# A decoder step on one core: the output projection cut in two halves, one among attention's steps, the other by thirds of the tokens

## The chip, the cores and the metric

One Trainium2 chip, one of its cores. A core has TensorE (PE, with its weight load PEld), VectorE (DVE), ScalarE (ACT), GpSimd (POOL) and SyncE (SP), which here only issues transfers. The metric is the time of one execution on the device, in microseconds. The inputs are in the chip's memory before it starts, the outputs there when it ends.

## The reference

One layer of a decoder for 1,024 prompt tokens with 16 learned tokens in front, and for 8 sequences that each add one token to 1,024 cached ones. All are computed together as T = 1,048 tokens of D = 2,048 channels, in float32.

```python
def rmsnorm(x, g):
    y = xf * lax.rsqrt(jnp.mean(xf * xf, axis=-1, keepdims=True) + RMS_EPS)
    return y * g
# h = h + W_out [ pool_branch(n) ; attn_branch(n) ],  n = RMSNorm(h), and at the end a final RMSNorm
u, z_pool, q, k, v, z_attn, qi, ki, wi = jnp.split(hn @ w_in, cuts, axis=-1)
# pool branch: (mean of the last 2/4/8/16 of u) - u, per group a linear map, scale, * silu(z_pool)
# attention branch: indexer scores pick 256 keys for each query; softmax over these with a penalty that
# grows with distance; output * silu(z_attn).  8 heads of 128, 2 groups of keys and values
y = rmsnorm(h + jnp.concatenate([pool, attn], -1) @ w_out, final_norm_g)
```

The two halves of the operand of w_out, 1,024 rows each, come from the pool branch (done long before attention) and from attention. The outputs are y, the new keys and values, and the new state of the pool branch.

## The kernel before

The tokens are 9 tiles of 128 (the last has 24: 16 of the prompt, 8 samples). Each engine runs a list of instructions of its own, written by hand; they wait for each other by counting semaphores (`wait_ge`). Nothing is scheduled by a compiler: the order in the text is the order on the engine.

**Split products.** A float32 product is made of three: every weight w is split in whi (by ACT, `split_hi`, L313) and the rest wlo (by DVE, `split_lo`, L323), every operand likewise in hi and lo, and PE adds whi x hi, whi x lo and wlo x hi. A projection goes by blocks of 128 output channels: SP loads a block of weights in two halves of 512 KB (wraw, a ring of 4), `project` (L331) runs its 16 steps of 128 input channels, `step` (L346) its three products for three chunks of tokens (350, 350, 348). That is 144 matmuls a block, gathered in three PSUM banks; ACT copies them to stage (`evacuate`, L486) and stores them in memory.

**Stages in order of time.** Input norm and the turning of x into ahi and alo, with two chunks of projection block 0 among the tiles by the table `EARLY` (L362); the indexer's queries, the indexer with main blocks among its heads; the main blocks, beside which DVE picks the top 256 keys; keys and values turned; prompt attention; attention of the 8 samples over cached pages; output projection; last norm. The part of PE's time up to 1270 us is, apart from the start, not touched.

**Prompt attention.** 18 units (`AUNITS`: tiles 8 to 0, key groups 0 and 1) of 4 heads, so 72 heads k. For head k PE computes the scores (`scores`, L1647 and L1666: three products per chunk, up to 1,040 keys), DVE adds bias and mask and finds the maximum (L1335) into a buffer prob (NPROB = 3 of them), ACT takes the exponential (L996), DVE or ACT divides. LAG = 7 heads later come its turned blocks: PE transposes 4 heads x 128 keys (L1700), ACT copies them to pts (L984), PE weighs the values with them (`weighted`, L1670, L1680, two PE passes a block) into out_bank(v), one of two banks, and DVE multiplies the unit's sum by the gate (`gate`, L1311). `back_blocks` (L514) says which blocks fall to which head. Keys and values are copied from PSUM into one tile each, kvtok (L1296), by ACT and DVE in turn.

**Output projection.** SP loads the operand's 16 rows of blocks back from memory (mix_scratch) into orow; ACT (`operand_hi`, L1006, L1009) and DVE (`operand_lo`, L1360, L1362) split them into oparts, 4 among the samples' steps, 12 after. Then 16 blocks: 144 matmuls, ACT's evacuation (L496, L498), PE's turning of the block before (`turn_h`, L1778: 8 transposes L1789 and 1 L1794), DVE's addition of x (`add_residual`, L1392), ACT's squares (L1043), and the store of h in memory (h_scratch). After the last block: DVE's roots, a reload of h, nine multiplications by root and weight (L1476) and the stores (L1099).

**Pages.** The samples' cached pages are loaded by SP (even halves) and POOL (odd halves) by `load_keys` and `load_values` (L466, L472); keys go to PSUM and are turned (L1729), scored (L1740), then softmax (exponential L1027), the turning of it (L1746) and the weighing of values (L1769).

## Time and profile before

| | |
|---|---|
| Median of three runs | 1995.37 us (1994.33, 1995.37, 1997.87) |
| Profiled execution | 1997.71 us |
| Its span, first to last instruction | 1996.0 us |
| Mean granted TensorE clock | 0.979 |
| Busy: PE, DVE, ACT, POOL | 94%, 47%, 29%, 11% |
| Moved by DMA over the whole span | 198.96 MB, 100 GB/s |

The profiled execution is one of its own. "Busy" is the time in which at least one instruction is under way on an engine; matmuls are pipelined, so that a PE which is always busy may still issue at less than its pace. The pace is read from the starts of instructions in a row. A row of the timeline groups equal instructions that follow each other; the time in square brackets is the idle time ahead of it and the instruction that ended it.

### The profile page before, as it was taken

What the parts mean: (1) busy time and instruction counts of PE and PEld (TensorE: products, weight loads), DVE (VectorE), ACT (ScalarE), POOL (GpSimd) and SP (SyncE); (2) the same over time, 40 slices, a digit from 0 to 9 for tenths busy, and PEclk for the clock granted to TensorE, in tenths of its full rate; (3) what the DMA queues carried; (4) which work ended last, traced back from release to release, by engine and by line L of the source; (5) the groups of instructions that cost most, each with busy time, mean ns of one, the idle gap of its engine ahead of it and who ended that gap; (6) DMA issues with size and microseconds to landing.
All of it is one profiled execution on the core that took longest, in us unless ns stands there. A gap on an engine that the chain in (4) does not pass through costs nothing.

```text
span 1996.0 us, 28168 instructions
## 1 busy us (share of the span) xinstructions
PE 1874.3 (94%) x11014; PEld 1702.9 (85%) x11014; DVE 941.1 (47%) x1549; ACT 582.6 (29%) x1094; POOL 221.6 (11%) x227
## 2 busy tenths in 40 slices
PE   5999989998999999999999999899988999999993
PEld 4899977867999999999999999666554699999993
DVE  7401038874666565556565656654542211111115
ACT  6211136751111221111111111466653312222221
POOL 5200000004000000314151610110012000000000
PEclk9999989999999999999999999999999999999996
DMA  6232133213222221323232322423348323333338
GB/s 214 57 90 75 53 85 84 67 35 96 83 75 66 64 74 55 122 76 116 82 112 85 112 85 86 128 73 92 93 139 267 107 66 86 85 85 87 94 95 341
DMA packets 245917, 198.96 MB, mean 100 GB/s; under 512 B 25332, under 2 KB 228028, under 8 KB 243507
## 3 DMA queue, kind: packets, MB, share of 16 engines
q1 hardware_dynamic: 214541, 134.51, 23.9%
q10 hardware_dynamic: 25990, 49.64, 6.7%
q0 software_dynamic: 5312, 13.83, 2.2%
q8 instruction: 45, 0.74, 0.2%
q14 instruction: 29, 0.24, 0.0%
HBM read 146.94 MB, written 51.46 MB: 99 GB/s over the span
## 4 chain that ended last, share of the span: by engine, by line
PE 83%; DVE 6%; ACT 4%; issue 2%; DMA 2%; SPq 1%; POOL 0%; DVEq 0%; ACTq 0%; POOLq 0%
PE ps L354 68%; PE ps L1680 3%; PE ps L1666 2%; PE ps L1549 2%; DVE score L1196 2%; PE ps L1740 2%; PE ps L1769 2%; ACT pts L984 1%; PE ps L1700 1%; PE ps L1620 1%; DVE fh L1476 1%; DVE alo L1121 1%; PE ps L1729 1%; ACT wraw L852 1%; PE ps L1789 1%
## 5 line engine op out<-in xcount | busy, mean ns | idle before, releaser
L328 DVE TENSOR_TENSOR wlo<-wraw,whi 128x1024 fp32r<-128x1024 f32 (+1 forms) x122 | 160.5, 1317 | 745.2 <-ACT whi L320 744.9
L354 PE MATMUL ps<-ahi,whi 128*128 128x350 f32 (+3 forms) x2160 | 474.2, 326 | 5.3 <-DVE wlo L328 3.0
L354 PE MATMUL ps<-alo,whi 128*128 128x350 f32 (+3 forms) x2160 | 471.4, 324 | 0.0
L354 PE MATMUL ps<-ahi,wlo 128*128 128x350 f32 (+3 forms) x2160 | 470.3, 323 | 0.0
L354 PEld LDWEIGHTS ps<-ahi,whi 128*128 128x128 f32 (+1 forms) x2160 | 367.3, 189 | 9.4 <-ACT stage L498 3.0
L354 PEld LDWEIGHTS ps<-alo,whi 128*128 128x128 f32 (+1 forms) x2160 | 368.5, 189 | 0.5
L354 PEld LDWEIGHTS ps<-ahi,wlo 128*128 128x128 f32 (+1 forms) x2160 | 367.7, 189 | 0.6
L354 PE MATMUL ps<-oparts,whi 128*128 128x350 f32 (+1 forms) x1536 | 290.5, 324 | 0.0
L320 ACT ACTIVATE whi<-wraw 128x1024 fp32r<-128x1024 f32 (+1 forms) x122 | 128.5, 1055 | 476.3 <-PE ps L354 379.4
L354 PEld LDWEIGHTS ps<-oparts,whi 128*128 128x128 f32 x1536 | 252.5, 189 | 1.1 <-DVE oparts L1362 0.2
L496 ACT ACTIVATE stage<-ps 128x700 f32<-128x700 f32 (+1 forms) x61 | 46.1, 756 | 611.9 <-PE ps L354 611.9
L1224 DVE MATCH_REPLACE8 score<-m,score 128x640 f32<-128x640 f32 (+6 forms) x224 | 204.3, 924 | 0.0
L1214 DVE MAX8 m<-score 128x8 f32<-128x640 f32 (+6 forms) x224 | 191.8, 927 | 16.1 <-POOL score L1838 15.8
L354 PE MATMUL ps<-oparts,wlo 128*128 128x350 f32 (+1 forms) x768 | 165.3, 323 | 0.0
L354 PEld LDWEIGHTS ps<-oparts,wlo 128*128 128x128 f32 x768 | 130.7, 189 | 0.0
L1680 PE MATMUL ps<-pts,kvtok 128*128 128x512 f32 (+1 forms) x180 | 85.9, 559 | 15.2 <-ACT pts L984 14.9
L1335 DVE CUSTOM_DVE_ANT_0 prob<-score,ps 16x1040 f32<-16x1040 f32 (+6 forms) x56 | 52.4, 935 | 71.3 <-PE ps L1666 71.1
L1549 PE MATMUL ps<-khi,qst 128*128 128x512 f32 (+3 forms) x208 | 62.7, 368 | 16.6 <-ACT wraw L852 10.8
L1196 DVE SCALAR_TENSOR_TENSOR score<-wraw,wsc,score 128x384 f32<-128x384 f32 (+6 forms) x56 | 56.0, 999 | 13.8 <-ACT wraw L852 9.7
L436 POOL DMA_DIRECT2D iload<-cache_idx_k x32 | 17.4, 546 | 403.0 <-issue 402.5
L1549 PEld LDWEIGHTS ps<-khi,qst 128*128 128x128 f32 (+1 forms) x208 | 31.8, 169 | 34.8 <-ACT wraw L852 14.3
L1196 DVE SCALAR_TENSOR_TENSOR score<-relub,wsc,score 128x384 f32<-128x384 f32 (+6 forms) x56 | 56.0, 999 | 10.6 <-ACT relub L852 5.8
(186 smaller groups left out, 1628.1 us busy)
## 6 DMA issues: line engine op xcount, KB each, us to landing
wraw<-w_in SPq DMA_DIRECT2D x88, 512.0 KB, 3.8
proj_scratch<-stage ACTq DMA_DIRECT2D x44, 524.0 KB, 2.7
wraw<-w_out SPq DMA_DIRECT2D x32, 512.0 KB, 6.1
orow<-mix_scratch SPq DMA_DIRECT2D x16, 524.0 KB, 5.8
xt<-x_prompt SPq DMA_DIRECT2D x7, 1024.0 KB, 4.9
xblk<-x_prompt SPq DMA_DIRECT2D x16, 448.0 KB
h_scratch<-hblk ACTq DMA_DIRECT2D x14, 512.0 KB
fh<-h_scratch SPq DMA_DIRECT2D x8, 896.0 KB, 11.2
```

Source lines behind the costliest of these rows:

```text
L320: nc.scalar.activation(whi[:, s, :, 0:width], wraw[:, 2 * p + s, :, 0:width], ACT.Copy).then_inc(S["w_hi"], 1)
L328: nc.vector.tensor_tensor(wlo[:, s, :, 0:width], wraw[:, 2 * p + s, :, 0:width], whi[:, s, :, 0:width].bitcast(F32), ALU.subtract).then_in ...
L354: last = nc.tensor.matmul(ps[0:width, 3 * pair(n) + c, 0:tn], w[:, s, k, 0:width], m[:, a, t0:t0 + tn], start=(a == 0 and w is whi and m i ...
L496: nc.scalar.activation(stage[0:width, p, 0:700].rearrange("p (c t) -> p c t", c=2), ps[0:width, b:b + 2, 0:350], f, scale=scale)
L1196: nc.vector.scalar_tensor_tensor(out=out, in0=relu_of(u)[0:rows, 0:keys_of(i)], scalar=wsc[0:rows, i, 8 * h + k:8 * h + k + 1], in1=out, o ...
L1214: x = nc.vector.max(m8[0:r, m, :], score_of(t)[0:r, :])
L1224: x = nc.vector.match_replace(score_of(t)[0:r, :], m8[0:r, m, :], score_of(t)[0:r, :], NEG_TAKEN)
L1335: nc.vector.tensor_tensor_reduce(x, dist_of(i)[0:n, :], psf[0:n, o:o + w], 1.0, NEG_TAKEN, ALU.add, ALU.max, peak).then_inc(S["abias"], 1)
L1549: last = nc.tensor.matmul(psf[0:rows, o + c:o + c + cw], qst[:, n % 2, k, 0:rows], m[:, c:c + cw], start=m is khi, stop=m is klo)
L1666: last = nc.tensor.matmul(psf[0:n, o + c:o + c + cw], q[:, qbuf(u), 4 * g + r, 0:n], m[:, g, c:c + cw], start=m is akh and q is qh, stop=q ...
L1680: nc.tensor.matmul(ps[:, out_bank(v), 0:4 * n], kvtok[0:kn, j, 256 + 128 * g:256 + 128 * g + 128], pts[0:kn, t % 2, 0:4 * n], start=j == 0 ...
L1740: nc.tensor.matmul(psf[0:64, c:c + w], q, skt[:, (m - 1) % 2, c:c + w], start=m == 1, stop=m == NSAMP * KVH)
```

## The change

**Start.** `EARLY` now puts two of three chunks of projection blocks 0 and 1 among tiles 3 to 9, and their third chunks behind the last tile. DVE and ACT split block 1 at tiles 4 and 5; block 0 has its split weights in buffers of its own (khi0, klo0).

```diff
-        EARLY = {3: (0, 0, 6), 4: (0, 6, 11), 5: (0, 11, 16), 6: (1, 0, 6), 7: (1, 6, 11), 8: (1, 11, 16)}
+        EARLY = {3: [(0, 0, 0, 6)],
+                 4: [(0, 0, 6, 11)],
+                 5: [(0, 0, 11, 16), (1, 0, 0, 8)],
...
+                 9: [(1, 1, 11, 16)]}
```

**First half of the output projection.** The rows of the pool branch (opart, 8 steps of 128) times w_out are cut in 384 fills: 16 blocks n x 3 chunks c (384, 384, 280 tokens) x 8 steps k, each three matmuls. 216 stand among the steps of prompt attention from head 8 on, 96 among the samples' steps, 72 behind them beside the split of the late operands. Eight fills make a part; all parts gather in PSUM bank 3, and each is copied by ACT into stage, a block's third part followed by the split of the weights after next and the store in part_scratch. One order for all engines is written by new functions:

```python
        AUNITS = [(i, g) for i in ATILES for g in range(KVH)]
        NHEAD = 4 * len(AUNITS)
        LAG = 6
...
        FILLS = [("fill", n, c, k) for n in range(NOUT) for c in range(len(OUT_CHUNKS)) for k in range(HALF)]
        IN_PROMPT, IN_SAMPLES = 216, 96
        def prompt_order():

            fills = FILLS[:IN_PROMPT]
            first = 8
            cost = [0 if k < first else 350 + (keys_of(AUNITS[k // 4][0]) if k < NHEAD else 100) for k in range(LAST_K)]
            order, waiting, done, t = [], None, 0, 0
            for k in range(LAST_K):
                order.append(("score", k))
                if waiting:
                    order.append(waiting)
                    waiting = None
                if k < HALF:
                    order.append(("operand", k))
                until = len(fills) * sum(cost[:k + 1]) // sum(cost)
                blocks = back_blocks(k)
                here, share = fills[done:until], max(1, len(blocks))
                done = until
                for x in range(share):
                    if x < len(blocks):
                        order.append(("turn", *blocks[x], t))
                    if x == 0:
                        order.append(("soft", k))
                    order += here[x * len(here) // share:(x + 1) * len(here) // share]
                    if x < len(blocks):
                        if waiting:
                            order.append(waiting)
                        waiting = ("weigh", *blocks[x], t)
                        t += 1
            assert not waiting
            return order
...
        def sample_order():

            fills = FILLS[IN_PROMPT:IN_PROMPT + IN_SAMPLES]
            order, done = [], 0
            for count, what in ([(3, ("keys", m)) for m in range(NSAMP * KVH + 1)] + [(17, ("probs", 0)), (4, ("copied", 0))]
                                + [(3, ("values", b)) for b in range(NSAMP)]):
                order += fills[done:done + count] + [what]
                done += count
            return order + fills[done:]

        def last_order():

            fills = FILLS[IN_PROMPT + IN_SAMPLES:]
            order = []
            for k in range(HALF):
                order += [("operand", k)] + fills[k * len(fills) // HALF:(k + 1) * len(fills) // HALF]
            return order
...
        def fill_act(act, n, c, k):

            if k < HALF - 1:
                return
            t0, tn = OUT_CHUNKS[c]
            act.wait_ge(S["o_mm"], 3 * n + c + 1)
            if c == 0 and n < 2:
                act.wait_ge(S["op_lo"], HALF)
            if c == 0 and n >= 2:
                act.wait_ge(S[f"stored{n % 2}"], 16 * (stored_blocks(n % 2) + n // 2))
            nc.scalar.activation(stage[:, n % 2, t0:t0 + tn], ps[:, 3, 0:tn], ACT.Copy).then_inc(S["o_kept"], 1)
            if c == len(OUT_CHUNKS) - 1:
                if n + 2 < NOUT:
                    out_hi(act, n + 2)
                else:
                    late_hi(act, n + 2 - NOUT)
                act.wait_ge(S["o_kept"], 3 * n + 3)
                act.dma_start(part_d[128 * n:128 * n + 128, :], stage[:, n % 2, :]).then_inc(S[f"stored{n % 2}"], 16)
...
        def fill_pe(pe, n, c, k):

            t0, tn = OUT_CHUNKS[c]
            if c == 0 and k == 0:
                pe.wait_ge(S["ow_lo"], n + 1)
            if n == 0 and c == 0:
                pe.wait_ge(S["op_lo"], k + 1)
                pe.wait_ge(S["abias"], 8)
            elif k == 0:
                pe.wait_ge(S["o_kept"], 3 * n + c)
            for w, x in ((whi, 0), (whi, 1), (wlo, 0)):
                last = nc.tensor.matmul(ps[:, 3, 0:tn], w[:, n % 2, k, :], opart[:, k, x, t0:t0 + tn],
                                        start=k == 0 and w is whi and x == 0, stop=k == HALF - 1 and w is wlo)
            if k == HALF - 1:
                last.then_inc(S["o_mm"], 1)
```

In attention the scores of even heads lie in banks 0 and 1 and those of odd heads in banks 4 and 5 (`score_bank`; only tile 8's 1,040 keys reach 16 columns into bank 2 or 3), the out bank is one (bank 2), the turned blocks use banks 6 and 7, prob has two buffers (NPROB = 2), the lag is 6. Blocks fall to three of a unit's four heads, and `gate(v)` stands in head 4 v + 10.

```diff
-                if j == 0 and v > 1:
-                    pe.wait_ge(S["gated"], v - 1)
+                if j == 0 and v:
+                    pe.wait_ge(S["gated"], v)
...
-                nc.tensor.matmul(ps[:, out_bank(v), 0:4 * n], kvtok[0:kn, j, 256 + 128 * g:256 + 128 * g + 128],
+                nc.tensor.matmul(ps[:, 2, 0:4 * n], vtok[0:kn, j, 128 * g:128 * g + 128],
```

The operand's eight rows are loaded and split in heads 0 to 7. Turned keys and values are copied by two instructions a tile, and the first two weight halves are split before the first head. Cached pages have whole tiles for themselves: the even samples come by SP, the odd by POOL, keys 0 and 1 early, the other keys and the values once all of attention's weighings are done.

The rows below are PE's order in prompt attention. Before, with kvtok for keys and values, pts the turned blocks and akh, qh the split keys and queries (L1700 turns, L1680 weighs, L1666 scores):

```order
3003 L1680 MATMUL ps<-pts,kvtok 128x512 [waits gated,pt_copied]
3004 L1700 MATMUL ps<-cst,prob 128x128 [waits pt_copied]
3005 L1700 MATMUL ps<-cst,prob 128x128 x3
3006 L1700 MATMUL ps<-cst,prob 128x128 [waits pt_copied]
3007 L1700 MATMUL ps<-cst,prob 128x128 x3
3008 L1680 MATMUL ps<-pts,kvtok 128x512 [waits pt_copied]
3009 L1666 MATMUL ps<-akh,qh 128x512 [waits abias]
```

PE in the same stage after the change (L1896 turns, L1910 weighs, L1882 scores, L695 is a fill; o_kept counts the parts that ACT has copied out of bank 3):

```order
2909 L1896 MATMUL ps<-cst,prob 128x128 [waits pt_copied]
2910 L1896 MATMUL ps<-cst,prob 128x128 x3
2911 L695 MATMUL ps<-opart,whi 128x384 x2
2912 L695 MATMUL ps<-opart,wlo 128x384
2913 L695 MATMUL ps<-opart,whi 128x384 x2
2914 L695 MATMUL ps<-opart,wlo 128x384
2915 L695 MATMUL ps<-opart,whi 128x384 [waits o_kept]
2916 L695 MATMUL ps<-opart,whi 128x384
2917 L695 MATMUL ps<-opart,wlo 128x384
2918 L1910 MATMUL ps<-pts,vtok 128x512 [waits gated,pt_copied]
2919 L1882 MATMUL ps<-akh,qh 128x512 [waits abias]
```

Between the transposes and the weighing stand fills now; the third of them is the first of a new part and waits for the copy of the part that ended one row before.

DVE at the first heads of attention, before (L1296 copies turned keys and values, L1335 is bias and maximum, prob its result):

```order
307 L1296 COPY kvtok<-ps 128x512 [waits kv_turned] x4
308 L1335 ISA prob,ast<-score,ps 16x1040 [waits aqk,dist_masked]
309 L1335 ISA ast 16x1
310 L1338 TENSOR_SCALAR ast<-ast 16x1 [waits abias]
311 L1335 ISA prob,ast<-score,ps 16x1040 [waits aqk]
312 L1335 ISA ast 16x1
```

and after (L631 is the weights' lower half, L1524 the operand's, L1570 bias and maximum):

```order
315 L1516 COPY vtok<-ps 128x256
316 L631 TENSOR_TENSOR wlo<-wraw,whi 128x1024 [waits ow_hi] x2
317 L1524 TENSOR_TENSOR opart<-stage,opart 128x1048 [waits op_hi,dist_masked]
318 L1570 ISA prob,ast<-score,ps 16x1040 [waits aqk]
319 L1570 ISA ast 16x1
320 L1573 TENSOR_SCALAR ast<-ast 16x1 [waits abias]
321 L1524 TENSOR_TENSOR opart<-stage,opart 128x1048 [waits op_hi]
322 L1570 ISA prob,ast<-score,ps 16x1040 [waits aqk]
```

One operand split stands ahead of each of the first heads' maxima.

**Second half.** The rows of attention (oattn) times w_out go by 48 parts: for each third of the tokens (384, 384, 280) all 16 blocks, 24 matmuls each, with the weights of a half block loaded again for each third (ring of 4). The stores and reloads of h are gone: DVE adds the first half's part (`join`), PE turns three transposes, DVE adds the result to x, which is already in fh; squares, roots, scaling and stores of a third run in the next third, those of the last behind the end.

```python
        def late_weights(q, j):

            if j < 2:
                q.wait_ge(S["ow_lo"], NOUT - 1 + j)
            elif j < 4:
                q.wait_ge(S["sv_used"], 3)
            else:
                q.wait_ge(S["lw_lo"], j - 3)
            n = j % NOUT
            q.dma_start(wraw[:, j % 4, :, :],
                        w_out[0, POOLW:D, 128 * n:128 * n + 128].rearrange("(k p) n -> p k n", p=128)
                        ).then_inc(S[f"w_in{j % 4}"], 16)
...
            for j in range(PARTS):
                c, n = divmod(j, NOUT)
                join(j)
                if j + 2 < PARTS:
                    late_lo(dve, j + 2)
                if j:
                    add_residual(j - 1)
                if c and n == 4:
                    moments(c - 1)
                if c and 5 <= n <= 7:
                    finish(3 * (c - 1) + n - 5)
            add_residual(PARTS - 1)
            moments(2)
            for i in tiles_of(2):
                finish(i)

...
            for j in range(PARTS):
                t0, tn = OUT_CHUNKS[j // NOUT]
                pe.wait_ge(S["lw_lo"], j + 1)
                if j >= 3:
                    pe.wait_ge(S["l_kept"], j - 2)
                for k in range(HALF):
                    if j == 0:
                        pe.wait_ge(S["oa_lo"], k + 1)
                    for w, x in ((whi, 0), (whi, 1), (wlo, 0)):
                        last = nc.tensor.matmul(ps[:, j % 3, 0:tn], w[:, j % 2, k, :], oattn[:, k, x, t0:t0 + tn],
                                                start=k == 0 and w is whi and x == 0, stop=k == HALF - 1 and w is wlo)
                    if k == 3 and j:
                        turn_h(j - 1)
                last.then_inc(S["l_mm"], 1)
            turn_h(PARTS - 1)
```

The end of PE's list before (L354 are the projection's matmuls, L1789 and L1794 turn the block before, stage holds what was evacuated):

```order
3799 L354 MATMUL ps<-oparts,wlo 128x348
3800 L1792 REGISTER_ALU
3801 L1794 MATMUL ps<-cst,stage 24x128 [waits h_part]
3802 L1805 REGISTER_ALU
3803 L1805 COMPARE_AND_BRANCH
3804 L1789 MATMUL ps<-cst,stage 128x128 [waits h_added,evac]
3805 L1789 MATMUL ps<-cst,stage 128x128 x7
3806 L1794 MATMUL ps<-cst,stage 24x128 [waits h_part]
```

and a part near the end after (L2024 the matmuls of a part, L2012 the transposes of the part before; lw_lo counts split weights, l_kept joined parts):

```order
5148 L2024 MATMUL ps<-oattn,whi 128x280 [waits l_kept,lw_lo]
5149 L2024 MATMUL ps<-oattn,whi 128x280
5150 L2024 MATMUL ps<-oattn,wlo 128x280
5151 L2024 MATMUL ps<-oattn,whi 128x280 x2
5152 L2024 MATMUL ps<-oattn,wlo 128x280
5153 L2024 MATMUL ps<-oattn,whi 128x280 x2
5154 L2024 MATMUL ps<-oattn,wlo 128x280
5155 L2024 MATMUL ps<-oattn,whi 128x280 x2
5156 L2024 MATMUL ps<-oattn,wlo 128x280
5157 L2012 MATMUL ps<-cst,stage 128x128 [waits h_added,l_kept]
5158 L2012 MATMUL ps<-cst,stage 128x128
5159 L2012 MATMUL ps<-cst,stage 24x128
5160 L2024 MATMUL ps<-oattn,whi 128x280 x2
```

A part waits only for its split weights and for the join of three parts before.

## Rows read from the trace of the kernel before

**Rows 1.** The page: span, and busy time of each engine.
```profile
span 1996.0 us, 28168 instructions
...
PE 1874.3 (94%) x11014; PEld 1702.9 (85%) x11014; DVE 941.1 (47%) x1549; ACT 582.6 (29%) x1094; POOL 221.6 (11%) x227
```
**Rows 2.** Windows: stretch, us, PE, PEld, DVE, ACT, POOL busy, clock, DMA, GB/s.
```profile
1282.90:1301.60 18.70, 16.50 (x99) 8.49 (x97) 16.77 (x40) 14.24 (x24) 6.11 (x12) 0.99 0.66 204
1301.60:1481.70 180.10, 165.09 (x801) 109.03 (x800) 99.05 (x329) 121.28 (x255) 7.26 (x13) 1.00 0.31 86
1481.70:1575.30 93.60, 86.82 (x392) 40.05 (x392) 12.06 (x12) 26.06 (x30) 20.34 (x38) 0.95 0.58 184
1575.30:1960.50 385.20, 385.20 (x2439) 383.60 (x2439) 73.65 (x103) 97.67 (x324) 0.00 (x0) 1.00 0.35 104
1960.50:1996.10 35.60, 1.48 (x10) 0.95 (x9) 23.99 (x27) 7.95 (x40) 0.00 (x0) 0.57 0.85 341
```
**Rows 3.** The chain that ended last: start, us, 72 matmuls of half a block.
```profile
1611.15 11.57 PE ps L354 x72
```
**Rows 4.** Timeline of PE, input stage: start, us, instruction, [idle before <-releaser].
```profile
43.84 1.76 PE L1492 MATMUL ps<-cst,xt 128*128 128x128 f32 x12 [0.35 <-DVE alo L1121]
...
49.36 1.76 PE L1492 MATMUL ps<-cst,xt 128*128 128x128 f32 x12 [0.36 <-DVE alo L1121]
```
**Rows 5.** Timeline of DVE: the first head's maximum, and an operand split.
```profile
1282.86 1.22 DVE L1335 CUSTOM_DVE_ANT_0 prob<-score,ps 16x1040 f32<-16x1040 f32 x1 [3.77 <-PE ps L1666]
...
1526.88 1.25 DVE L1362 TENSOR_TENSOR oparts<-orow,oparts 128x1048 fp32r<-128x1048 f32 x1 [4.64 <-ACT oparts L1009]
```
**Rows 6.** Attention: timelines of PE, ACT and DVE, then PE's grouped rows.
```profile
1323.07 0.57 PE L1666 MATMUL ps<-akh,ql 128*128 128x512 f32 x2
1323.48 1.02 PE L1680 MATMUL ps<-pts,kvtok 128*128 128x512 f32 x2
1324.33 1.04 PE L1700 MATMUL ps<-cst,prob 128*128 128x128 f32 x8
1325.62 1.12 PE L1680 MATMUL ps<-pts,kvtok 128*128 128x512 f32 x2 [0.25 <-ACT pts L984]
...
1322.74 1.15 ACT L1004 ACTIVATE prob<-prob,ast 128x1024 f32<-128x1024 f32 x1
1324.97 1.08 ACT L984 ACTIVATE pts<-ps 128x512 f32<-128x512 f32 x2 [1.08 <-PE ps L1700]
...
1323.67 1.09 DVE L1335 CUSTOM_DVE_ANT_0 prob<-score,ps 128x896 f32<-128x896 f32 x1 [2.49 <-PE ps L1666]
1325.07 0.75 DVE L1309 TENSOR_SCALAR prob<-prob,ast 128x1024 f32<-128x1024 f32 x1
...
L1680 PE MATMUL ps<-pts,kvtok 128*128 128x512 f32 x144 | 78.7, 628 | 13.2 <-ACT pts L984 13.2
L1700 PE MATMUL ps<-cst,prob 128*128 128x128 f32 x288 | 40.1, 273 | 0.0
L1666 PE MATMUL ps<-akh,qh 128*128 128x512 f32 x44 | 25.9, 610 | 0.0
```
**Rows 7.** Timeline of ACT at two places, then PE's waits in the samples' stage.
```profile
1534.25 1.24 ACT L1027 ACTIVATE sprob<-sprob,sst,cst 64x1025 f32<-64x1025 f32 x1 [5.42 <-DVE sst L1371]
1581.17 1.08 ACT L1009 ACTIVATE oparts<-orow 128x1048 fp32r<-128x1048 f32 x1 [1.85 <-DMA orow<-mix_scratch]
...
PE ps L1746 <- DVE sprob L1376: 5.1, 1, 5.1
```
**Rows 8.** Timelines of ACT and DVE in the tail.
```profile
1961.18 0.46 ACT L498 ACTIVATE stage<-ps 128x348 f32<-128x348 f32 x1
...
1970.09 20.44 DVE L1476 SCALAR_TENSOR_TENSOR fh<-fh,fst,fg 128x2048 f32<-128x2048 f32 x9
```
**Rows 9.** DMA queues, 1575 to 1961 us: packets, MB, share of 16 engines.
```profile
q1 hardware_dynamic: 50017, 32.72, 28.8%
```

1123 lines of the change are left out of this document (592 added, 531 removed).

## Prediction

> **What bounds the kernel now.** I read the busy times of the page first: PE is busy for 1874.3 of 1996.0 us, DVE and ACT for 47% and 29% [rows 1]. The change touches what comes after 1282.9 us and the input stage, so I cut the span there by stages [rows 2]. The output projection (1575.3 to 1960.5) has PE busy in all of its 385.2 us, and the tail behind it only for 1.48 of 35.6 us: there is nothing to win in the first but by moving its matmuls under the idle time of other stages, and much in the second. Prompt attention (1301.6 to 1481.7) shows PE at 165.1 of 180.1 us, but a busy PE there is not a full one. The timeline [rows 6] gives true pitches from start to start: four score matmuls (512 and 384 columns twice) begin 0.41 us apart for 896 columns, 0.457 ns a column, so 0.234 us for 512, 0.175 for 384, 0.128 for 280; a weighing (two records of 512) takes 0.85, a transpose record 0.109. By the counts of the grouped rows, 72 weighings are 61, 288 transposes 31, the scores of 512, 384, 256 and 128 columns 31 + 8.4 + 5.6 + 2.8, the small ones of the last tiles 7: 147 us of work in 180, so 33 us are lost. Where: after its last transpose PE waits for ACT's copy (the weighing at 1325.62 comes 0.42 us later than 1324.33 + 8 x 0.109) and restarts slowly. The samples' stage summed likewise has 76 us of work in 93.6, 18 lost, 5.1 of them the wait for the softmax [rows 7]. In the output projection 72 matmuls take 11.57 us [rows 3], or 0.161 each, which is its full pitch. Durations are from the profiled execution, 1997.71 us; the median of the runs is 2.3 lower, and the sum is made against 1997.71.
>
> **The change, part by part.** The count of matmul columns in the output projection does not change: 16 blocks x 16 steps x 3 products x 1048 columns in both, 0.478 us for a step's three products over 350 or so columns, and the three new chunks (0.525 + 0.525 + 0.385) average the same. What changes is what else PE does meanwhile.
>
> (a) *Start.* Before, PE idles between input tiles: two starts of a tile's transposes are 5.5 us apart [rows 4], with 1.76 of transposes and some 2.6 of block 0 in it, so about 1.1 is free in each. The new table puts two thirds of block 1 there (32 steps, 32 x 3 x 0.16 = 15.4 us), more than is free in six tiles (7 us); what doesn't fit lengthens the stage, and the rest comes off behind it. DVE's block 1 split moves too. I take -3, between -5 and +1.
>
> (b) *Keys, values and the first eight heads.* Each turned tile is copied by two instructions instead of one, and four weight splits stand between them and the first head: +2. Then each of the first eight heads gets one operand half-split: 1.08 us on ACT and 1.25 us on DVE [rows 5, 7]. DVE is busy for 16.77 of 18.70 us in this stretch [rows 2], and so it sets the pace: the DVE part stands on the path, 8 x 1.25 = 10, less 1 that fits in its idle time: +9. Together +11; the bounds are +6 (the rest of DVE's idle time and the longer lead of scores take half) and +15 (ACT too, at 14.24, becomes late).
>
> (c) *Rest of attention.* 216 of the 384 fills stand between the turns and the weighings. A fill lasts 0.5 us and the wait it covers 0.42, so the 33 us lost go: -33. In return all fills accumulate in one PSUM bank, so the first fill of each part waits until ACT has copied the part before. There are 27 such places here; in 16 a fill stands right behind a fill, as in the second order excerpt (the wait for o_kept). The copy takes 0.46 us [rows 8], the last matmul's drain and PE's restart about 0.3 more, so 0.7 with ACT free. But ACT is busy for 121.3 of 180.1 us [rows 2], in pieces of 1.15 (exponential) and 1.08 (copy of turned blocks) [rows 6], and each copy has its fixed place in ACT's order: 67% of about 1.1 in front, plus what stands before it in the order. I take 1.7 each, 27 us, and 2 for the 11 separated ones: +29. With one output bank in place of two, the first weighing of a unit also waits for DVE's gating of the unit before, placed in the same head: 17 times about 0.5, as DVE is at 55% here: +8. Sum +4. If ACT is always ahead, it is 16 x 0.7 + 2 x 0 and a hidden gate, -33 + 13 = -20; if each wait takes a whole piece of ACT's work more (2.8), +20.
>
> The order excerpt shows the wait and [rows 2] an ACT that is busy for 67%. The Trainium skill, Perfetto Trace Analysis, section Matmuls, speaks against this change: independent groups of matmuls should rotate through different PSUM banks, so that the evacuation of one overlaps the matmuls of the next, and here the parts share one. By that rule alone the price is one copy and its restart a part, which is rival A's value; no row of before shows either.
>
> (d) *Samples.* 96 fills go among 76 us of work: the 18 lost go, and 12 part ends cost 0.7 each, ACT being nearly idle (26.06 of 93.6 us [rows 2]): +8. One of them stands behind ACT's exponential of the softmax, which waits for DVE: +3. The changed page loads and the start cost +3. Sum -4, between -12 and +6.
>
> (e) *The last nine parts.* 72 fills now stand with eight late operands. 8 boundaries in a row: 8 x 0.7 = 6. The first operand can only be split after the last value matmul, the gated output's way through memory being as long as now (orow lands, ACT waits 1.85, [rows 7]): 7.3 us against 3.8 us of fills that do not wait on ACT, so +4. Sum +10, between +6 and +16.
>
> (f) *The second half by thirds.* 48 parts of 24 matmuls and three transposes, 199 us of PE work in all. The third excerpt shows the only waits: the split weights and the joined part. Per part (4.5 us) ACT has 1.05 and DVE 1.3 of splitting, 0.5 of join and 0.4 of residual; with two or three finishing multiplications of 2.27 (20.44 / 9, [rows 8]) in a third DVE can be late. The queue must bring 25 MB of weights (each half block of 512 KB three times), 8.6 MB of parts and 8.6 MB of x, and beside them 5.7 MB of finished rows go out, less some 2 MB loaded ahead: 46 MB in 199 us, 231 GB/s. The row of the stage now: q1 moves 32.72 MB with 28.8% of 386 us [rows 9], that is 294 GB/s while it moves. It should do, but x's 3.1 MB burst per third stands in front of weights in the same queue (10.6 us against a ring of four parts, 17 us). I take +6, from 0 to +25.
>
> (g) *Tail.* Now 35.6 us, 20.44 of it nine scalings in a row, behind a reload of h [rows 2, 8]. After, three scalings stand there and no reload: -6 x 2.27 = -13.6, and 1.5 for the reload's share: -15, between -12 and -18.
>
> Sum: -3 + 11 + 4 - 4 + 10 + 6 - 15 = **+9**: 2006.7 for a profiled run, 2004 for the median.
>
> **Rivals.** *A, the waits stay small and it is faster.* If PE's deep queue of other work keeps ACT ahead, part ends cost 0.7 and gates nothing: (c) is -20 and (d) -8, and (b) half hidden at +9: -3 + 9 - 20 - 8 + 8 + 4 - 14 = -24, and 7 for late parts, so -17: 1981 profiled, 1978 for the median. For it: PE has 3.4 fills or 1.6 us more in each of 64 heads, so that ACT, with 27 copies and 9 blocks' splits added (121 + 12 + 10 us of some 255), falls from 67% to 56%. Against it: an in-order ACT queue in which the copy stands behind pieces that themselves wait for PE. *B, transfers bound the thirds and it is slower.* If weights arrive at less than 231 GB/s, PE waits for splits in every part; at 200 GB/s 46 MB take 230 us: +31 instead of +6, and so 2029. Against it: 294 GB/s in the row. It decides from 231 GB/s down. *C, DVE rather than PE bounds attention*, as in the first eight heads: DVE's work in the rest is 99 of 180 us [rows 2], plus 14 splits of 1.23 and nothing else, so it does not bind. *D, it does nothing*: the gains and the stalls of (c) cancel with (b) and (g) to under 4 us, as when a part end in attention costs 1.3 us and not 1.7 (16 x 0.4 = 6 us less).
>
> **How the numbers follow.** Forecast (slower by 4 to 20 us, centre 2004) 0.39; A 0.38; B 0.11; D 0.12; C is inside the forecast's bounds. A measurement of this kernel can tell about 0.2%, 4 us, from no change: slower 0.50 (forecast and B), same 0.12 (D), faster 0.38 (A). The range takes in A with 10 us more (d and e at their lower bounds) and so begins at 1968, and B with a queue at 203 GB/s (+28), 2026; outside lie less than 0.1 on either side. The likeliest case by itself spans 1999 to 2016.
>
> **What would show it.** In the trace after: (b) DVE's reductions of the first eight heads 3.4 us apart, not 2.3; (c) PE's first fill of a part idle for ACT's copy, 25 to 30 us in total over attention, and weighings idle for DVE's gate under 10; if the first is under 12, A is right. (e) a gap of 4 us at the first matmul of the second half's operand. (f) PE waiting for wlo, with transfers in flight, only at the starts of thirds; if in each part, B. (g) about 20 us from PE's last matmul to the end. My forecast is wrong if attention's stretch with its fills (147 + 103 us of work) lasts under 260 us, or if the thirds last over 215.

## The result, and the profile after

The changed kernel takes 2032.76 us, the median of four runs (2029.88 to 2034.64), against 1996.62 us for the kernel before in the same comparison: a ratio of 1.0167, with a 95% interval of 1.0149 to 1.0186. It is slower by 36 us. The sign of the forecast was right, but "slower" had been given a chance of 0.50 only. Its size (+9 us on the profiled run, 2004 us) was not right, and the time lies outside the range of 1968 to 2026.

The page of the changed kernel, its span and busy times, which answer to [rows 1]:

```profile
span 2032.9 us, 27737 instructions
...
PE 1887.0 (93%) x11014; PEld 1711.4 (84%) x11014; DVE 1003.9 (49%) x1641; ACT 595.2 (29%) x885; POOL 220.6 (11%) x227
```

The windows of its stages (us, PE, PEld, DVE, ACT, POOL busy, granted clock, DMA share, GB/s) answer to [rows 2]:

```profile
1282.20:1326.30 44.10, 29.48 (x133) 19.43 (x131) 25.01 (x47) 23.22 (x38) 0.00 (x0) 0.69 0.46 146
1326.30:1618.50 292.20, 266.53 (x1426) 213.40 (x1426) 108.72 (x338) 141.00 (x284) 7.32 (x14) 0.99 0.28 80
1618.50:1756.60 138.10, 130.79 (x663) 81.69 (x663) 9.89 (x15) 28.71 (x39) 27.19 (x51) 1.00 0.43 135
1756.60:1800.50 43.90, 36.55 (x217) 34.23 (x218) 12.63 (x13) 13.38 (x18) 0.00 (x0) 1.00 0.58 184
1800.50:2017.60 217.10, 204.32 (x1298) 200.51 (x1296) 119.70 (x175) 67.85 (x69) 0.00 (x0) 0.98 0.73 222
2017.60:2032.90 15.30, 0.03 (x1) 0.00 (x0) 8.65 (x12) 2.37 (x7) 0.00 (x0) 0.64 0.41 150
```

The windows start at the same landmarks as those of before: the first maximum of head 0, the maximum of head 9, the first matmul of the samples' bias, the end of the samples' values, the last fill, PE's last transposes. To compare, the fills in a stretch are taken off at 0.478 us each (there are 4, 218, 90.3 and 71.7 of them in the first four), and the second half is held against what is left of the old projection, 385.2 - 384 x 0.478 = 201.6 us.

| stretch | before | after less fills | difference | forecast |
|---|---|---|---|---|
| to the first turned key | 1270.0 | 1267.9 | -2.1 | (a) -3 |
| to head 0's maximum | 12.9 | 14.3 | +1.4 | (b) +2 |
| heads 0 to 8 | 18.7 | 42.2 | +23.5 | (b) +9 |
| rest of attention | 180.1 | 188.0 | +7.9 | (c) +4 |
| samples | 93.6 | 94.9 | +1.3 | (d) -4 |
| last nine parts | 0 | 9.6 | +9.6 | (e) +10 |
| second half | 201.6 | 217.1 | +15.5 | (f) +6 |
| tail | 35.5 | 15.3 | -20.2 | (g) -15 |
| sum | | | +36.9 | +9 |

The largest row is the first heads (the stretch of 18.7 us in [rows 2] holds nine heads, 0 to 8; the prediction counted eight). From one maximum to the next, heads 0 to 7 took 14.0 us before and 28.0 after, and the step from head 7 to head 8 took 1.8 and 11.4. The chain of work that ended last passes through them as follows (start, us, what):

```profile
1282.36 3.37 DMA stage<-mix_scratch
1285.75 1.09 ACT opart L1193
1286.86 1.25 DVE opart L1524
1288.11 1.14 DVE prob L1570
...
1292.88 1.17 ACT prob L1230
1294.05 0.97 ACT opart L1193
1295.04 1.25 DVE opart L1524
1296.29 1.14 DVE prob L1570
```

It is not DVE's 1.25 us alone that lies on the path, as the prediction had it, but a loop over both engines: DVE's maximum waits in DVE's order for the operand's low half, that for ACT's high half, and that in ACT's order for a normalisation, which waits for DVE. From 1285.75 to head 6's maximum the chain holds five of DVE's subtractions (6.1 us) and three of ACT's copies (3.0 us). Then, from head 7 to head 8, DVE stands for 9.9 us with nothing to do, and PE's clock has fallen. In windows of 5 us of the same kernel (columns as above; the figure third from the end is the granted clock, 0.50 being the lower of its two levels, 1.2 GHz):

```profile
1285.00:1290.00 5.00, 2.50 (x15) 0.89 (x14) 4.17 (x9) 3.84 (x5) 0.00 (x0) 1.00 0.56 157
...
1300.00:1305.00 5.00, 1.00 (x8) 0.92 (x8) 2.77 (x6) 3.48 (x6) 0.00 (x0) 0.50 0.31 107
1305.00:1310.00 5.00, 4.24 (x17) 2.61 (x18) 3.97 (x7) 1.19 (x2) 0.00 (x0) 0.50 0.17 41
1310.00:1315.00 5.00, 3.98 (x21) 3.49 (x20) 1.45 (x4) 2.62 (x6) 0.00 (x0) 0.50 1.09 337
1315.00:1320.00 5.00, 5.00 (x19) 3.89 (x19) 0.00 (x0) 1.58 (x4) 0.00 (x0) 0.50 0.75 263
1320.00:1325.00 5.00, 5.00 (x20) 4.64 (x20) 2.19 (x5) 1.45 (x3) 0.00 (x0) 0.50 0.02 5
```

The kernel before is at 1.00 in all of these windows. In windows of 1 us the fall lies near 1298.4 us, and the clock is back at 1.00 near 1325.7, after 27 us. PE had been busy for a little under half of the 13 us before the fall, and had stood for 3.2 us just ahead of it:

```profile
1297.49 0.65 PE L1882 MATMUL ps<-akh,qh 128*16 128x512 f32 x3 [3.20 <-DVE ast L1570]
...
1297.00:1298.00 1.00, 0.51 (x3) 0.23 (x4) 0.93 (x5) 1.00 (x3) 0.00 (x0) 1.00 0.66 163
1298.00:1299.00 1.00, 1.00 (x7) 0.38 (x6) 1.00 (x2) 1.00 (x2) 0.00 (x0) 0.69 0.90 356
```

The same scores of head 8 in the two kernels, before (L1666) and after (L1882):

```profile
1314.55 0.62 PE L1666 MATMUL ps<-akl,qh 128*128 128x512 f32 x2
1315.01 0.62 PE L1666 MATMUL ps<-akh,ql 128*128 128x512 f32 x2
...
1315.12 1.05 PE L1882 MATMUL ps<-akl,qh 128*128 128x512 f32 x2
1315.97 1.05 PE L1882 MATMUL ps<-akh,ql 128*128 128x512 f32 x2
```

Two matmuls of 512 columns take 0.46 us before and 0.85 after.

Part ends. The timelines of PE and ACT where a part ends with ACT occupied, and where ACT is free:

```profile
1412.22 0.33 PE L695 MATMUL ps<-opart,wlo 128*128 128x384 f32 x1
1412.56 1.03 ACT L1222 ACTIVATE prob<-prob,ast 128x896 f32<-128x896 f32 x1
1413.59 0.48 ACT L659 ACTIVATE stage<-ps 128x384 f32<-128x384 f32 x1
1414.12 0.53 PE L695 MATMUL ps<-opart,whi 128*128 128x280 f32 x2 [1.57 <-ACT stage L659]
...
1796.38 0.34 PE L695 MATMUL ps<-opart,wlo 128*128 128x384 f32 x1
1796.75 0.49 ACT L659 ACTIVATE stage<-ps 128x384 f32<-128x384 f32 x1 [3.60 <-PE ps L695]
1797.30 0.53 PE L695 MATMUL ps<-opart,whi 128*128 128x280 f32 x2 [0.58 <-ACT stage L659]
```

The next fill starts 1.90 us after the last one in the first case and 0.92 in the second, where 0.175 would do: 1.7 and 0.75 us lost. Those are the two values of the prediction (1.7 and 0.7). The mean lies between them: at the 16 places in this stretch where a fill follows a fill across a part end, measured like this, 20.1 us are lost, 1.3 each. The rule that the prediction named (the Trainium skill, Perfetto Trace Analysis, section Matmuls: independent groups should rotate through PSUM banks, so that a copy overlaps the next group's matmuls) agrees with the trace: 0.75 us is lost at a part end even where ACT is free. ACT's own work comes on top of it. PE's waits in the rest of attention, then in the last nine parts (us in total, times, longest):

```profile
PE ps L695 <- ACT stage L659: 22.4, 20, 2.2
PE ps L1910 <- DVE osb L1548: 2.6, 3, 1.3
...
PE ps L695 <- ACT stage L659: 7.4, 8, 3.3
```

(The restart after a wait is not in the idle time.) The single output bank costs 2.6 us, not 8: fills stand in front of that wait too. In the last nine parts one wait of 3.3 us is the late operand's.

Thirds. Parts begin every 4.53 us in the whole second third and every 3.42 us in the last, the pitch of their matmuls. The first third has three parts of 8.73, 11.16 and 7.37 us. What stands there, timelines of PE, DVE and ACT:

```profile
1818.67 0.55 PE L2012 MATMUL ps<-cst,stage 128*128 128x128 f32 x3 [2.45 <-DVE stage L1633]
...
1817.52 0.56 DVE L1645 TENSOR_TENSOR fh<-ps,fh 128x384 f32<-128x384 f32 x1 [5.50 <-DMA fh<-x_prompt]
...
1820.32 1.06 ACT L641 ACTIVATE whi<-wraw 128x1024 fp32r<-128x1024 f32 x1 [9.56 <-DMA wraw<-w_out]
```

x is late for DVE, and the weights behind x for ACT. PE waits only twice for split weights (7.8 us in total), both times in the first third.

### The profile page after: what moved, and what is told of

Its sections match the earlier page's. It is cut to its first block, busy times and chain, and to the rows that moved or that the text cites. A ratio compares the mean times of both kernels' runs of the same rounds, so it can differ in the third digit from the quotient of the medians.

```text
span 2032.9 us, 27737 instructions
## 1 busy us (share of the span) xinstructions
PE 1887.0 (93%) x11014; PEld 1711.4 (84%) x11014; DVE 1003.9 (49%) x1641; ACT 595.2 (29%) x885; POOL 220.6 (11%) x227
## 4 chain that ended last, share of the span: by engine, by line
PE 81%; DVE 6%; ACT 4%; DMA 4%; issue 3%; SPq 2%; POOL 0%; DVEq 0%; ACTq 0%; POOLq 0%
PE ps L350 49%; PE ps L695 9%; PE ps L2024 7%; PE ps L1910 3%; PE ps L1882 3%; PE ps L1770 2%; PE ps L1896 2%; PE ps L1953 1%; DVE score L1415 1%; PE ps L1979 1%; PE ps L1841 1%; ACT stage L659 1%; DMA wraw<-w_out 1%; PE ps L1942 1%; ACT wraw L1063 1%
## 5 line engine op out<-in xcount | busy, mean ns | idle before, releaser
L350 PE MATMUL ps<-ahi,whi 128*128 128x350 f32 (+1 forms) x2112 | 463.8, 326 | 5.1 <-DVE wlo L328 2.7
L350 PE MATMUL ps<-alo,whi 128*128 128x350 f32 (+1 forms) x2112 | 461.5, 324 | 0.0
L350 PE MATMUL ps<-ahi,wlo 128*128 128x350 f32 (+1 forms) x2112 | 460.2, 324 | 0.0
L350 PEld LDWEIGHTS ps<-ahi,whi 128*128 128x128 f32 x2112 | 361.3, 190 | 8.6 <-ACT stage L507 3.0
L350 PEld LDWEIGHTS ps<-alo,whi 128*128 128x128 f32 x2112 | 362.3, 190 | 0.0
L350 PEld LDWEIGHTS ps<-ahi,wlo 128*128 128x128 f32 x2112 | 361.8, 190 | 0.0
L328 DVE TENSOR_TENSOR wlo<-wraw,whi 128x1024 fp32r<-128x1024 f32 x88 | 119.4, 1358 | 448.8 <-ACT whi L319 448.6
L695 PE MATMUL ps<-opart,whi 128*128 128x384 f32 (+1 forms) x768 | 205.0, 352 | 36.1 <-ACT stage L659 36.1
L319 ACT ACTIVATE whi<-wraw 128x1024 fp32r<-128x1024 f32 x88 | 93.3, 1061 | 379.1 <-PE ps L350 358.2
L1433 DVE MAX8 m<-score 128x8 f32<-128x640 f32 (+6 forms) x224 | 191.8, 926 | 16.1 <-POOL score L2058 15.8
L2024 PE MATMUL ps<-oattn,whi 128*128 128x384 f32 (+1 forms) x768 | 187.1, 330 | 7.8 <-DVE wlo L646 7.8
L695 PEld LDWEIGHTS ps<-opart,whi 128*128 128x128 f32 x768 | 128.3, 191 | 56.9 <-ACT stage L659 34.8
L2024 PEld LDWEIGHTS ps<-oattn,whi 128*128 128x128 f32 x768 | 132.5, 190 | 8.7 <-DVE wlo L646 8.5
L1570 DVE CUSTOM_DVE_ANT_0 prob<-score,ps 16x1040 f32<-16x1040 f32 (+6 forms) x56 | 52.3, 934 | 152.5 <-PE ps L1896 92.2
L695 PE MATMUL ps<-opart,wlo 128*128 128x384 f32 (+1 forms) x384 | 124.8, 325 | 0.0
L2024 PE MATMUL ps<-oattn,wlo 128*128 128x384 f32 (+1 forms) x384 | 124.2, 323 | 0.0
L641 ACT ACTIVATE whi<-wraw 128x1024 fp32r<-128x1024 f32 x48 | 50.9, 1061 | 144.1 <-PE ps L2024 119.6
L1910 PE MATMUL ps<-pts,vtok 128*128 128x512 f32 (+1 forms) x180 | 83.1, 545 | 6.6 <-DVE osb L1548 2.6
L631 DVE TENSOR_TENSOR wlo<-wraw,whi 128x1024 fp32r<-128x1024 f32 x16 | 19.5, 1224 | 136.7 <-ACT whi L626 136.7
```

Source lines behind the costliest of these rows:

```text
L319: nc.scalar.activation(hi[:, s, :, 0:width], wraw[:, 2 * p + s, :, 0:width], ACT.Copy).then_inc(S["w_hi"], 1)
L328: nc.vector.tensor_tensor(lo[:, s, :, 0:width], wraw[:, 2 * p + s, :, 0:width], hi[:, s, :, 0:width].bitcast(F32), ALU.subtract).then_inc( ...
L350: last = nc.tensor.matmul(ps[0:width, 3 * pair(n) + c, 0:tn], w[:, s, k, 0:width], m[:, a, t0:t0 + tn], start=(a == 0 and w is hi and m is ...
L641: nc.scalar.activation(whi[:, j % 2, :, :], wraw[:, j % 4, :, :], ACT.Copy).then_inc(S["lw_hi"], 1)
L695: last = nc.tensor.matmul(ps[:, 3, 0:tn], w[:, n % 2, k, :], opart[:, k, x, t0:t0 + tn], start=k == 0 and w is whi and x == 0, stop=k == H ...
L1433: x = nc.vector.max(m8[0:r, m, :], score_of(t)[0:r, :])
```

## The experiments

Seventeen kernels ran beside the kernel before. Times below are medians of four runs; a comparison was made against the kernel before on the same chip, whose median is given with it. That median lies between 1996.6 and 2003.3 us from one comparison to the next. A difference between two changed kernels that were compared apart is therefore good to some 5 us, and small ones are given by their ratios as well (0.001 is 2 us).

### Part ends pulled apart

```diff
-            return order
+            return separated(order)
...
+                if item[0] == "fill":
+                    held.append(item)
+                else:
+                    out.append(item)
+                    since += cost.get(item[0], 0)
+                while held and (held[0][3] or since >= GAP):
+                    out.append(held.pop(0))
+                    since = 0.0
```

(`held[0][3]` is the fill's k, 0 at the start of a part; GAP is 0.8 us; `cost` is 1.0 for scores, 0.85 for a weighing, 0.44 for a turn, 2.0 for page keys and values.)

> The changed kernel with its part ends pulled apart: the first fill of a part is held back until at least 0.8 us of other PE work (scores, turns, weighings, page keys, values) has been issued behind the last fill of the part before; the later fills move with it. Nothing else is changed. Theory (one PSUM bank: PE stands at each part end for ACT's copy and what ACT has queued before it): the stalls between two fills, 37 us in attention and 11 in the samples' stage in the trace of the changed kernel, fall to under half, and the time by 15 to 28 us, to about 2010. Rival (ACT's queue is the limit, so that the wait reappears at the next instruction): under 5 us gained.

2018.47 us, before 1997.61, ratio 1.0097 (1.0075 to 1.0119): 14.3 us less than the changed kernel, just under the expected range. Of this 9.8 us lie between heads 8 and 71. PE's waits for ACT's copy in attention fell from 22.4 us to

```profile
PE ps L712 <- ACT stage L676: 8.8, 14, 1.3
PE ps L1927 <- DVE osb L1565: 7.4, 6, 2.6
```

and some of it came back as the wait for the gate in the second row. The single bank is a cost of the order, more than of the bank.

### The operand's low half on POOL

```diff
-                nc.vector.tensor_tensor(opart[:, k, 1, :], orow1[:, k % 2, :], opart[:, k, 0, :].bitcast(F32),
+                nc.gpsimd.tensor_tensor(opart[:, k, 1, :], orow1[:, k % 2, :], opart[:, k, 0, :].bitcast(F32),
```

> The changed kernel with the eight subtractions that make the low half of the pool operand moved from DVE to POOL, which is idle there. Theory (the 1.25 us on DVE are on the path of the first heads): the step from head to head in heads 0 to 7 falls from 4.0 to about 2.8 us, 8 to 10 us gained there, minus what POOL's slower subtraction holds back (the reload of the next operand row waits for it). Rival (ACT's high halves and the loads set that pace, DVE only waits): under 3 us.

2028.72 us, before 1997.61, ratio 1.0150 (1.0128 to 1.0172), 4 us less, within the two intervals, and far under the 8 to 10 expected. Heads 0 to 7 took 25.9 us and not 28.0, and the step to head 8 stayed at 11.4. The chain shows another loop in the old one's place:

```profile
1286.07 2.44 POOL opart L2099
...
1288.53 3.53 DMA stage<-mix_scratch
...
1292.08 1.08 ACT opart L1193
...
1293.23 2.41 POOL opart L2099
```

The operand's rows pass through two buffers. A new row is loaded only when the subtraction from its buffer is done, and POOL takes 2.4 us for it where DVE took 1.25. The round of subtraction, load and ACT's copy takes 7.2 us for two rows. Up to head 6 this kernel was 6.7 us ahead, then head 7 came 10.5 us behind head 6 and not 5.9: its scores stand in PE's order behind a weighing that waits for ACT's copy of a turned block, and this copy stands in ACT's order behind the operand's, which waits for its row. So this run does not tell DVE's share: it exchanged one loop for another.

### Two buffers in the kernel before

```diff
-NPROB = 3
+NPROB = 2
...
-        LAG = 7
+        LAG = 6
...
-            return [(v, j) for j in quarter(AUNITS[v][0], r)]
+            if v >= len(AUNITS) or r == 3:
+                return []
+            i = AUNITS[v][0]
+            return [(v, j) for j in range(r * (i + 1) // 3, (r + 1) * (i + 1) // 3)]
```

> The kernel before with two prob buffers instead of three, a lag of 6 heads instead of 7, and a unit's turned blocks in three heads instead of four, as the change has it; no fills, no operand work. Theory (head 4u must wait until the unit two before is wholly turned, which ends only in that head): 8 us lost from head 7 to head 8, and some 0.5 to 1.5 us at each of 15 later units: 1996 + 8 + 15 = about 2019, 2010 to 2030. Rival (the two buffers cost nothing by themselves, only beside fills): within 4 us of before.

2011.58 us, before 1997.61, ratio 1.0075 (1.0047 to 1.0103): 14 us slower, inside the expected range. Maximum of head 0 to that of head 8 went from 15.8 to 22.3 us, from there to head 71 from 175.3 to 183.8. DVE's waits in attention show what the buffer does; the first row, for PE's turns, is not there at all in the kernel before:

```profile
DVE prob L1338 <- PE ps L1703: 69.9, 16, 7.9
DVE prob L1338 <- PE ps L1669: 23.4, 19, 3.2
```

Sixteen times DVE cannot begin a unit until PE has turned the unit two before. The edit holds three things, the buffers, the lag and the order of the turns, and they were not run apart. In heads 0 to 8 there is a fourth: after a wait of 1.8 us the clock was at 0.50 here too, from 1295 to 1298 us. The prediction gave NPROB and LAG no term.

### No fills among attention and samples

```diff
-        IN_PROMPT, IN_SAMPLES = 216, 96
+        IN_PROMPT, IN_SAMPLES = 0, 0
```

> The changed kernel with no fills in attention and in the samples' stage: all 384 stand behind them, with the late operands. Theory (fills cover PE's waits in attention and in the samples' stage, 34 + 18 us before, but pay 0.75 us at a part end and more behind ACT's work): 48 part ends in a row cost 36 us and the cover is lost, so about 2064, 2050 to 2080. Rival (fills among attention cost as much as they cover): 2025 to 2045.

2093.34 us, ratio 1.0477 (1.0453 to 1.0501), 60 us more than the changed kernel and more than expected. The 384 fills in a row take 227.6 us, 44 more than their pitch. Attention from head 8 to 71 takes 216.7 us without any fill, against 175.3 before and 183.8 in the kernel with two buffers. The step from head 7 to head 8 takes 9.0 us here and 11.4 with its two fills. The windows of the rest of attention and of the fills:

```profile
1315.80:1537.00 221.20, 181.48 (x772) 117.58 (x773) 97.09 (x317) 121.57 (x252) 4.64 (x8) 0.92 0.22 60
1630.90:1858.50 227.60, 197.79 (x1154) 184.57 (x1154) 28.19 (x26) 43.74 (x70) 0.00 (x0) 0.99 0.30 97
```

The clock is lower (0.92), and PE's waits for the gate, 2.6 us with fills, are 16.9:

```profile
PE ps L1910 <- DVE osb L1548: 16.9, 12, 2.5
```

The change's new attention is bad alone and good as a bed for fills: 203 fills (97 us) stand in the changed kernel between heads 8 and 71, and lengthen this by only 281.9 - 216.7 = 65 us.

### The operand's split ahead of attention

The rows are loaded into opart's low half, as the last main block leaves that memory, and split in place.

```diff
+            sp.wait_ge(S["w_used"], 2 * B_OUT - 1)
+            for k in range(4):
+                load_operand(k)
...
+                else:
+                    for k in range(4):
+                        operand_hi(k)
...
-                if k < HALF:
-                    order.append(("operand", k))
+                if k < 2:
+                    order.append(("operand", k + 6))
```

> The changed kernel with the pool operand's split moved ahead of attention: its rows are loaded straight into opart as soon as the last main block has left that memory, four of eight are split while the last main block runs, two beside the turning of keys and values, two in heads 0 and 1. Theory (ACT's high halves, their loads and DVE's low halves pace heads 0 to 7, at 4.0 us a head against 2.0 before): those seven steps fall from 28 to 17 us, which is what the kernel before with two prob buffers took, and the time by 8 to 11 us, to about 2023. Rival (the wait for the turned unit sets when head 8 starts, whatever came before): the step from head 7 to 8 grows from 11.4 us by as much, under 3 us gained.

2024.57 us, before 2003.31, ratio 1.0116 (1.0091 to 1.0140); its profiled span is 10.6 us shorter than the changed kernel's. Heads 0 to 7 fell from 28.0 to 18.6 us, near the 17.2 of the kernel with two buffers; the step to head 8 stayed at 11.4. This is the clean price of the split in the first heads, 9.4 us. The theory held, its rival fell.

### x in quarters

```diff
-            load_x(0)
+            load_x(0, 0)
...
-                if j == 1:
-                    load_x(1)
+                if j in (0, 2, 4):
+                    load_x(0, j // 2 + 1)
+                if j in (6, 8, 10, 12):
+                    load_x(1, j // 2 - 3)
```

> The changed kernel with the loads of x for each third cut in four column quarters of 512 channels, issued between the weights of the parts before them instead of 3 MB at once ahead of weights. The bytes are the same. Theory (a burst in front of the weights in SP's queue starves parts 3, 5 and 6 of the first third; the queue's mean rate is enough): the first third falls from 86.2 us to about 74, the time by 9 to 13 us. Rival (the thirds are short of transfer rate altogether): the same 13 us spread over more parts, under 4 us gained.

2020.18 us, before 2003.31, ratio 1.0091 (1.0071 to 1.0111); the span is 14.4 us shorter. The first third takes 72.4 us, its full pitch, with the same bytes:

```profile
1799.80:1872.20 72.40, 72.39 (x432) 71.56 (x431) 34.44 (x45) 17.30 (x17) 0.00 (x0) 1.00 0.91 266
```

At 266 GB/s nothing waits. Rival B of the prediction (too little transfer rate) falls; it was the order in SP's queue.

### Two banks for the last nine parts

```diff
+            p = 3 * n + c
+            return 7 if p >= LATE and (p - LATE) % 2 == 0 else 3
...
-                pe.wait_ge(S["o_kept"], 3 * n + c)
+                pe.wait_ge(S["o_kept"], 3 * n + c - (1 if 3 * n + c > LATE else 0))
```

> The changed kernel with two PSUM banks in turn (7 and 3) for the last nine parts of the first half, where bank 7 is free; a part's first fill then waits for the copy of the part before the last. Theory (the 0.75 us at each part end are the drain and the copy in the one bank): the 9.5 us lost in these nine parts fall to 3 or 4 (the late operands in ACT's order remain), 5 to 7 us gained, about 2026. Rival (ACT's place in the order sets it): 0 to 2 us.

2021.34 us, before 2003.31, ratio 1.0098 (1.0075 to 1.0122). From the last value matmul to the last fill 35.8 us pass and not 45.3, the pitch of the fills within 1.5 us: all 9.5 lost there are gained, the late operand's wait with them, more than expected. The span is 13.1 us shorter; the other 3 lie before 1270 us, where the two programs are the same, and are scatter.

### All four

> All four repairs at once in the changed kernel: part ends pulled apart (14.3 us gained alone), the pool operand split ahead of attention, x in quarters, two banks for the last nine parts. If the causes are separate, their gains add: 2032.8 - 14 - 9 - 11 - 6 = about 1993, 1987 to 2000, level with the kernel before. If they overlap (one wait taking the other's place) it stays above 2003.

1988.06 us, before 2003.31, ratio 0.9936 (0.9915 to 0.9957): faster than the kernel before. Spans shortened by 16.1, 10.6, 14.4 and 13.1 us add to 54, together they gave 46.8; medians shortened by 14.3, 8.2, 12.6 and 11.4 add to 46.5, together they gave 44.7. The spans contain the scatter of the stages ahead, which is the same program in most of these kernels: head 0's maximum comes between 1279.3 and 1283.6 us. The causes are separate to within that scatter.

### A unit turned in two heads, alone and with all four

```diff
-            if v >= len(AUNITS) or r == 3:
+            if v >= len(AUNITS) or r >= 2:
...
-            return [(v, j) for j in range(r * (i + 1) // 3, (r + 1) * (i + 1) // 3)]
+            return [(v, j) for j in range(r * (i + 1) // 2, (r + 1) * (i + 1) // 2)]
...
-            v, r = divmod(k - LAG - 4, 4)
+            v, r = divmod(k - LAG - 3, 4)
```

> The changed kernel with a unit's blocks turned in two heads (4v+6 and 4v+7) instead of three, and its gate one head earlier. Theory (head 4u on DVE waits, with two prob buffers, for the last turned block of the unit two before, which the change's order puts in that very head, behind fills): the step from head 7 to 8 falls from 11.4 us to about 4, the 15 later steps of that kind by 1 to 3 us each as far as PE waits for them; 7 to 15 us gained, about 2020. Rival (PE has fills to do meanwhile, only the first such step costs): 3 to 7 us.

2028.08 us, before 1997.34, ratio 1.0157 (1.0140 to 1.0174): 4.7 less than the changed kernel, the rival's range, but 2 by the ratios, whose intervals overlap. In the traces the step from head 7 to head 8 fell to 8.3 us and not to 4, heads 0 to 7 grew by 1.3, and heads 8 to 71 took 5 us less. DVE's 103.6 us of waits for turns are gone; they had been free for the most part.

> All four repairs (1988 us) and the two-head turning of units. Theory as for that alone, on a kernel whose other stalls are gone: 1988 - 5 to 10 = 1978 to 1983. Rival (with its other stalls gone, PE's larger groups of turns wait for ACT's copies): 1988 or above.

1978.03 us, before 1997.34, ratio 0.9911 (0.9895 to 0.9928), 10 less than the four repairs by the medians and 5 by the ratios; the next kernel, on the same chip, is 6.8 us slower than this one.

### A wider gap at part ends

GAP = 1.3 instead of 0.8, with the four repairs.

> All four repairs with the first fill of a part held back by 1.3 us of other PE work instead of 0.8. Theory (the stalls left at part ends, 8.9 us of idle PE in attention to the last fill, are those where ACT has a piece of 1.1 us in front of the copy): 3 to 5 us gained, 1983 to 1985. Rival (held fills leave later turns uncovered): 0 or slower.

1984.83 us, ratio 0.9936 (0.9920 to 0.9953); the four repairs had the same ratio on another chip. No gain is shown.

### The old table at the start

```diff
-                 5: [(0, 0, 11, 16), (1, 0, 0, 8)],
+                 5: [(0, 0, 11, 16)],
...
+                 9: [(1, 0, 0, 16), (1, 1, 0, 16)]}
```

> The changed kernel with the old table at the start: two chunks of block 0 among tiles 3 to 8, all of block 1 behind the last tile. Theory (the free time between input tiles takes some of block 1's matmuls): 3 us lost, about 2036. Rival (the earlier matmuls only push the input tiles back): within 1 us.

2038.79 us, before 1997.34, ratio 1.0207 (1.0190 to 1.0224), 6 us more, twice what was expected. The first key is turned at 1274.9 us, 7 later than in the changed kernel and 5 later than before. The early split of block 1 stays in this kernel, and tiles 5 and 6 begin 7.0 us after the tile ahead of them instead of 5.5, which is 3 of the 5. The early chunks gain 7 and what came with them costs 5; that the split causes all 5 is not shown.

### Matmuls that nobody reads, for the clock

```diff
+                if k < 6:
+                    for _ in range(DUMMY):
+                        nc.tensor.matmul(ps[0:n, 7, 0:BANK], qh[:, (u // KVH) % 2, 4 * g + r, 0:n], akh[:, g, 0:BANK],
+                                         start=True, stop=True)
```

> The changed kernel with six matmuls of 512 columns that nobody reads behind each of the first six heads' scores, to keep PE busy there (1.4 us a head at full clock, into a bank that is free). Theory (PE is busy for only half of 1285 to 1300 us, the granted clock falls to 0.5 from 1300 to 1325, and PE's work of heads 6 to 9 takes twice as long): the clock stays at or near 1.0, the step from head 7 to 8 falls from 11.4 us to 6 or 7, and the time falls by 6 to 10 us in spite of the added work. Rival (the order of operand splits and the two prob buffers set that step, the clock is a bystander): the step stays above 10 us, and the time does not fall.

2035.12 us, before 1999.05, ratio 1.0179 (1.0153 to 1.0205): no gain. PE stood for 3.3 us up to 1301.2, and from 1301 to 1324 us the clock was at 0.50; the step from head 7 to 8 was 11.4 us.

> The changed kernel with the operand's split moved ahead of attention, and the same unread matmuls in heads 0 to 5. Theory (clock): against 2024.6 us without them 6 to 9 us less, and heads 0 to 8 in about 22 us, as in the kernel before with two prob buffers (22.3). Rival: no change, or slower by the added work.

2027.18 us, ratio 1.0141 (1.0114 to 1.0167), as without them or slower. The clock held to 1310 us; the step was 9.9 us and not 11.4, but heads 0 to 7 took 21.0 instead of 18.6.

To fill the two waits as well:

```diff
+                if t == 0:
+                    unread(6, 14)
...
+                    pe.wait_ge(S["abias"], 6)
+                    unread(3, 12)
                     pe.wait_ge(S["abias"], 7)
```

> The kernel of a_warm with unread matmuls also where PE stood next: 14 of 480 columns before the first turn, in the turn's own free bank, and 12 before the first weighing, in bank 3, while PE waits there anyway. Theory (clock): the granted clock is at 1.0 from 1285 to 1320 us, the step from head 7 to 8 falls from 11.3 to 6 or 7 us, and the time is 4 to 8 us under a_warm's 2035.1. Rival (the waits between engines set the step, not PE's speed): the clock is up, the step stays above 10.

2032.92 us, before 1998.85, ratio 1.0171 (1.0154 to 1.0188). The clock is up to 1308.7 us, and falls nevertheless, within a wait that is left (the first row is PE's):

```profile
1309.42 0.69 PE L1925 MATMUL ps<-pts,vtok 128*128 128x64 f32 x2 [1.80 <-ACT pts L1208]
...
1300.00:1305.00 5.00, 4.66 (x33) 2.90 (x34) 4.16 (x7) 2.88 (x7) 0.00 (x0) 1.00 0.01 3
...
1310.00:1315.00 5.00, 5.00 (x18) 3.83 (x18) 0.00 (x0) 1.33 (x3) 0.00 (x0) 0.50 1.09 380
```

The step from head 7 (1306.6 us) to head 8 (1317.4) was 10.8 us, and PE was at the low level for all but its first 2. So these kernels do not answer the question they were made for: none kept the clock up through that step. They show that a fall in head 8's neighbourhood does not need the idle time of heads 0 to 6; it then comes with a later wait. The other part of the step is plain in all of them: the last turn of unit 0 stands in PE's order behind the scores of head 8 and two fills, and with two buffers DVE waits for it.

### Fills in the first heads

```diff
-            return 7 if p >= LATE and (p - LATE) % 2 == 0 else 3
+            return 7 if p < 3 or p >= LATE and (p - LATE) % 2 == 0 else 3
...
-                until = len(fills) * sum(cost[:k + 1]) // sum(cost)
+                until = 4 * min(k + 1, 6) + (len(fills) - 24) * sum(cost[:k + 1]) // sum(cost)
```

> The best kernel so far (four repairs and two-head turning, 1978 us) with real work in place of unread matmuls: the first 24 fills (three parts) stand in heads 0 to 5 in bank 7, which is free until the first turn. Theory (clock, and idle PE that can be filled): 24 x 0.48 = 11 us of fills leave later stretches, heads 0 to 8 take at most 3 us more, the clock stays up: 10 to 15 us gained, about 1966. Rival (the fills only lengthen the first heads): 1975 to 1980.

1971.17 us, before 1999.05, ratio 0.9856 (0.9830 to 0.9882), 7 less than without by the medians and 11 by the ratios. Heads 0 to 8 grew by 8.9 us and not 3, and the stretch behind them shrank by 12. The clock fell here too, to 0.50 from 1306 to 1320, but it fell in the kernel without these fills as well (1297 to 1310), and the step from head 7 to 8 is the same in both (8.8 and 8.7). The growth lies ahead of it: 10.9 us up to head 6, before the clock fell, for 11.5 us of fills, of which 2 came back up to head 7. With 8 and 12 unread matmuls in its two waits:

> The best kernel (c_fill0, 1971 us) with 8 unread matmuls before the first turn and 12 before the first weighing. Theory (clock): PE idles there from 1302.7 to 1305.6 us and the clock is at 0.5 from 1308 to 1318; with it kept up, heads 7 and 8 take 3 to 4 us less in all, about 1968. Rival: same time or slower.

1971.33 us, before 1998.85, ratio 0.9864 (0.9848 to 0.9881), the same. c_fill0 and this one are the fastest kernels of the study, 28 us under the kernel before and some 62 under the change as it was made.

## Why the prediction was wrong, step by step

Of the 28 us between +9 and +36.9, 14 are (b)'s, 9.5 are (f)'s, 5 are (d)'s and 4 are (c)'s; (g) took 5 back. (b), at 24.9 us in all, lies far outside its bounds of +6 to +15, and (g) 2 us below its own; the others are inside.

**Right.** The sign, at a chance of 0.50. (a) -3 against -2.1, the copies of (b) +2 against +1.4, and (e) +10 against +9.6. The two prices of a part end, 0.7 and 1.7 us, are both in the trace (0.75 and 1.7); the 0.3 us for drain and restart in the first had no row behind it. Their mean, 1.3 and not 1.7, was mis-sized: 20.1 us at 16 part ends against 27. (g) had the right mechanism and was 5 us short: after its transposes the old tail did more than the reload, and a third is left of the scalings (6.87 us against 20.44 [rows 8]) and of the squares.

**(b), heads 0 to 8: +23.5 instead of +9.** This is the step that failed. The prediction took the operand's split for the only cost of these heads. That term had nearly the right size: moving the split ahead gave back 9.4 us. Its reason, "it sets the pace: the DVE part stands on the path", is half of it, for the chain goes through ACT's copies too. That 9 and 9.4 agree is partly luck: fewer of DVE's subtractions on the path than eight, and ACT's beside them.

The other 14 us had no term at all. Two buffers instead of three, with the lag and the order of turns that came with them, cost 6.6 us in heads 0 to 8 of the kernel before, 3 us of that stretch at the lower clock. Some 7.5 us remain, and 6.2 of them lie in the step from head 7 to head 8: 11.4 us against 5.1 in the kernel before with two buffers. Two fills are 2.3 of it (9.0 us without fills). The granted clock has a part in what is left, at 0.50 for 27 us: pitches are nearly double there (0.85 against 0.46 us). How much was not isolated, for no kernel kept the clock up through that stretch; the bound from the windows is half of PE's 19.2 busy us between 1300 and 1325, 9.6, if all of it were on the path. This stays open.

**(c), rest of attention: +7.9 instead of +4,** inside its bounds, but by other terms than forecast: part ends 20 and not 29 us, the gate 2.6 and not 8, since fills stand ahead of it, and two buffers, 8.5 us in the kernel before, without a term. With the 33 us of cover these come to about -2, so some 10 us of loss in this stretch have no cause shown. How much the buffers cost beside fills is not shown either: when DVE's waits for turns were taken away, this stretch gained 5 us. (The lower bound of (c) adds 13 where 16 x 0.7 is 11.)

**(d) +1.3 instead of -4,** inside its bounds. PE idles for 6.3 us at part ends, 7.7 with the restarts, against 8 forecast; so the other losses of the stage did not all vanish. Which of them stayed is not shown.

**(f) +15.5 instead of +6,** inside its bounds. The mechanism was named (x ahead of weights in one queue) and mis-sized: "10.6 us against a ring of four parts" took one burst of 3.1 MB, but the second one follows it after one part, 6.3 MB in a stretch in which the ring was just filling. The proof is the same bytes in another order at 72.4 us.

**The chances.** Rival A's condition (ACT ahead) did not come about; rival B's rate was there (266 GB/s without a wait), its price came from the order. D's condition did come about (1.3 us a part end), and its outcome did not, because of (b) and (f). Of the signs that the prediction gave, PE's idle time for ACT's copy was 22.4 us against 25 to 30, the gate under 10, the late operand's wait 3.3 against 4; the first heads stood 4.0 us apart and not 3.4, and the thirds lasted 217.1 us, over the 215 that it gave as a sign of being wrong. Range and forecast missed because the change's plan of buffers and of PE's order in the first heads, and the clock there, had no term, and because (f) took one burst for two.

## What to carry to other kernels

A buffer that goes from three to two is a term of its own: ask which instruction of which engine must be over before the buffer's next first write, and where it stands in that engine's order. Work that is put on two engines in turn is priced along the loop through both, and moving one half to a third engine can open another loop, as the operand's rows on POOL did. And where a filler accumulates in a single bank, let other work stand behind each part's end; that alone was 14 us here, and ordering the loads by need another 13.

## What the runs showed of the hardware

The granted clock fell to 0.50 at the start of attention in the changed kernel, in nine of its variants, and in the kernel before with two buffers, and every time inside a wait of PE or within 1.4 us behind it. These waits were of 3.2 us (the changed kernel, and without fills), 3.3 (a_warm), 2.9 (c_fill0), 2.7 (a_opearly, c_turn2), 1.8 (a_warm2, b_two), 1.5 (o_warm, c_warm2) and 8.8 (a_poollo). In the kernel before no wait of PE there is longer than 0.9 us, and its clock stays at 1.00. A wait of 1.7 us in the changed kernel, before 1292.65, was not followed by a fall, so the wait alone does not decide it. Matmuls that nobody reads moved the fall by 3 to 14 us and did not prevent it, and the low stretch lasted between 3 us (b_two) and 48 us (a_nofill). The turns and weighings of the first unit, which follow these waits, are all of 16 to 64 columns.

POOL took 2.4 us for the float32 subtraction of 128 x 1048 that DVE does in 1.25 us.

The queue that moved 294 GB/s while it moved in the old projection [rows 9] is not limited to that. The DMA view of the changed kernel from 1803 to 1832 us, where x and weights queue (GB/s in 40 slices of 0.7 us, then q1's packets, MB and share):

```profile
GB/s 145 0 57 305 338 158 282 350 260 283 203 237 328 441 407 418 441 376 359 345 305 300 319 309 298 389 430 383 413 452 395 418 452 395 418 452 396 418 452 301
...
q1 hardware_dynamic: 4145, 9.62, 95.0%
```

9.62 MB in 95% of 29 us are 349 GB/s, and the last 14 slices of 383 to 452, some 10 us, average 419. The Trainium skill, DMA: Bandwidth & Descriptors, Specifications, gives about 358 GB/s as the limit of a core towards memory; the mean of the queue stays under it, those 10 us do not, so for one core running alone the measurement decides against taking it as a ceiling.
